# Scores of two heads issued together, a rounded forget bias, and fewer unread products in a softmax stage

## The reference

```python
# forgetting branch (per layer)
c = jnp.cumsum(log_f, axis=1).transpose(0, 2, 1)          # one row of 256 sums per head
z = jnp.einsum('bthd,bshd->bhts', q, k) * scale
z = z + cb[..., None] - c[:, :, None, :]                   # forget bias
p = jax.nn.softmax(jnp.where(causal, z, -jnp.inf), axis=-1)
...
# sparse branch (per layer)
z = jnp.einsum('btgrd,btkgd->btgrk', q, k_sel) * scale
p = jax.nn.softmax(jnp.where(valid, z, -jnp.inf), axis=-1)
...
# sliding-window attention (second block)
s = jnp.einsum('bnqkgd,bnskd->bnkgqs', q, kb) * (SWA_HEAD_DIM ** -0.5)
s = jnp.where(mask, s + bias, -jnp.inf)
p = jax.nn.softmax(jnp.concatenate([s, sink], -1), axis=-1)[..., :-1]
```

## Time and profile before

| | us |
|---|---|
| median of 3 runs | 2611.24 (2606.49 to 2626.17) |
| the profiled execution | 2605.32 |
| its span | 2603.5 |
| TensorE busy | 2487.0 (96%) |
| VectorE busy | 1755.4 (67%) |
| ScalarE busy | 1419.3 (55%) |
| mean granted TensorE clock | 0.977 |

### The profile page before, as it was taken

One profiled execution on the slowest core, in us unless ns is written; L12 is line 12 of the kernel. 1 busy time (PEld: TensorE's weight loads), 2 busy tenths in 40 slices (PEclk: granted clock), 3 DMA queues, 4 the chain that ended last, 5 costly groups with the idle time before them and its releaser, 6 DMA issues. The chain is left out here.

```text
span 2603.5 us, 34769 instructions
## 1 busy us (share of the span) xinstructions
PE 2487.0 (96%) x13881; PEld 2106.1 (81%) x13881; DVE 1755.4 (67%) x2013; ACT 1419.3 (55%) x1625; POOL 136.5 (5%) x176
## 2 busy tenths in 40 slices
PE   6999999999998999999999897999999999999996
PEld 6786789888866998878899786888888888888885
DVE  3345655544466555666544557898989898988987
ACT  3543544454345444523434445777777777777775
POOL 0101200001022000042000000000000000000000
PEclk9999999999999999899999997999999999999998
DMA  8232355532424455604555426999999999999996
GB/s 282 98 135 97 131 187 178 193 138 102 161 99 162 170 194 179 116 1 133 173 181 194 138 65 203 365 367 365 358 364 366 360 359 362 365 356 358 368 363 226
DMA packets 391569, 586.60 MB, mean 225 GB/s; under 512 B 21168, under 2 KB 284656, under 8 KB 391280
## 3 DMA queue, kind: packets, MB, share of 16 engines
q1 hardware_dynamic: 391408, 584.37, 66.3%
HBM read 580.13 MB, written 4.19 MB: 224 GB/s over the span
## 5 line engine op out<-in xcount | busy, mean ns | idle before, releaser
L3378 DVE TENSOR_TENSOR moe_low<-ring,moe_high 128x2048 fp32r<-128x2048 f32 x288 | 658.9, 2290 | 96.3 <-ACT moe_high L3339 92.4
L3339 ACT CAST moe_high<-ring 128x2048 fp32r<-128x2048 f32 x288 | 548.8, 1908 | 154.0 <-PE bank L3263 81.2
L3263 PE MATMUL bank<-moe_high,moe_xh 128*128 128x512 f32 x896 | 240.6, 390 | 7.9 <-PEq L3088 7.9
L3263 PE MATMUL bank<-moe_high,moe_xl 128*128 128x512 f32 x896 | 240.3, 390 | 0.0
L3263 PE MATMUL bank<-moe_low,moe_xh 128*128 128x512 f32 x896 | 240.1, 390 | 0.0
L3263 PEld LDWEIGHTS bank<-moe_high,moe_xh 128*128 128x128 f32 x896 | 168.4, 188 | 43.1 <-issue 8.1
L3263 PEld LDWEIGHTS bank<-moe_high,moe_xl 128*128 128x128 f32 x896 | 168.7, 188 | 35.2
L3263 PEld LDWEIGHTS bank<-moe_low,moe_xh 128*128 128x128 f32 x896 | 168.5, 188 | 35.1
L2048 DVE TENSOR_TENSOR chain_low<-ring,chain_high 128x2048 fp32r<-128x2048 f32 x48 | 110.0, 2292 | 127.3 <-ACT chain_high L2021 127.3
L2021 ACT CAST chain_high<-ring 128x2048 fp32r<-128x2048 f32 x44 | 83.8, 1904 | 151.9 <-PE bank L1992 116.9
L3269 PE MATMUL bank<-moe_high,moe_hh 128*128 128x512 f32 x448 | 128.4, 408 | 2.3 <-DVE moe_hl L3383 2.3
(11 more groups left out here) (513 smaller groups left out, 4993.6 us busy)
## 6 DMA issues: line engine op xcount, KB each, us to landing
ring<-in_moe_w_gate SPq DMA_DIRECT2D x199, 512.0 KB, 5.7
ring<-in_moe_w_up SPq DMA_DIRECT2D x199, 512.0 KB, 7.4
ring<-in_moe_w_down SPq DMA_DIRECT2D x95, 1024.0 KB, 7.9
ring<-in_w_in SPq DMA_DIRECT2D x22, 2048.0 KB, 8.0
ring<-in_w_down SPq DMA_DIRECT2D x14, 2048.0 KB, 7.9
ring<-in_w_up SPq DMA_DIRECT2D x10, 2048.0 KB, 8.1
xT<-in_moe_w_down SPq DMA_DIRECT2D x18, 1024.0 KB, 7.7
xT<-in_moe_w_gate SPq DMA_DIRECT2D x31, 512.0 KB, 5.7
```

The costliest lines, as they stand in the source:

```text
L3263: mm = pe.matmul(core.banks[i % 2][:], (xl if other_low else xh)[:, place(m), 4 * part + c, :], wt[:, c, :], start=(part == 0 and j == 0 a ...
L3339: act.copy(unit(high, u), ring.raw(u)).then_inc(s["weight_high"], 1)
L3378: dve.tensor_tensor(unit(low, u), ring.raw(u), unit(high, u), ALU.subtract)\
```

## The change

The scores of heads `i` and `i+1` are issued together on every even step: first both heads' products for the first 128 queries, then both for the second 128, so that neighbouring products use array rows 0 to 63 and 64 to 127 in turn. They wait until both banks are free. In the forget stage the two bias products of a half follow the two score products. A bias product is now of type fp32r with 72 array rows: the sums are held as three rounded parts (rows 0 to 7, 32 to 39, 64 to 71), and a matrix of zeros and ones, `thirds`, picks a head's three rows. VectorE makes those parts from 72 rows of sums, with four operations more at unit 21, two more at unit 17 and two more at unit 19. In the swa stage one unread product per step is left of four. `thirds` adds 8 columns to the constants, and `cum` has moved out of the arena.

The line numbers of the changed kernel are higher: L1180 are the scores, L1185 the bias products, L1079 the gate projection, L370 the unread products, L1200 the transposes, L1208 to L1210 the products with the values.

```diff
--- before.py
+++ after.py
@@ -44,7 +44,7 @@
 ARENA = 15232
-LOWER, UPPER, UPPER_BC = 7168, 6144, 5248
+LOWER, UPPER, UPPER_BC = 6976, 6144, 5248
 TRI = 3 * P
@@ -86,6 +86,7 @@
         "expert": np.tile(np.arange(E), (P, 1)),
+        "thirds": (p % 32 == np.arange(8)[None, :]) & (p < 72),
     }
@@ -1170,21 +1171,24 @@
         for i in range(heads + 3):
-            h = i
-            if h < heads:
-                if h >= 2:
-                    pe.wait_ge(s["masked"], h - 1)
-                bank = core.banks[h % 2]
+            if i < heads and i % 2 == 0:
+                both = (i, i + 1)
+                if i >= 2:
+                    pe.wait_ge(s["masked"], i)
                 for t, (a, b) in enumerate(edges):
-                    mm = pe.matmul(bank[:, a:b], q(h)[:, t * P:(t + 1) * P], k(h)[:, 0:b - a],
-                                   start=True, stop=(bias is None))
-                    if bias is not None:
-                        mm = pe.matmul(bank[:, a:b], bias_lhs(h), bias_rhs[:, 0:b - a], start=False, stop=True)
-                mm.then_inc(s["scores"], 1)
+                    for h in both:
+                        mm = pe.matmul(core.banks[h % 2][:, a:b], q(h)[:, t * P:(t + 1) * P], k(h)[:, 0:b - a],
+                                       start=True, stop=(bias is None))
+                        if bias is None and t == NT - 1:
+                            mm.then_inc(s["scores"], 1)
+                    for h in both if bias is not None else ():
+                        mm = pe.matmul(core.banks[h % 2][:, a:b], bias_lhs(h), bias_rhs[:, 0:b - a], start=False, stop=True)
+                        if t == NT - 1:
+                            mm.then_inc(s["scores"], 1)
             if logits is not None:
...
             if sink is not None:
-                idle_products(core, pe, core.banks[2 + i % 2][:, TRI:BANK], 4)
+                idle_products(core, pe, core.banks[2 + i % 2][:, TRI:BANK], 1)
             h = i - 2
@@ -1421,11 +1425,16 @@
     LOADS = 6
-
-    def __init__(self, core, rows, turned, fl, b, cum, tmp, logits):
-        self.core, self.rows, self.turned, self.fl, self.b, self.cum, self.logits = core, rows, turned, fl, b, cum, logits
+    ROWS = 72
+
+    def __init__(self, core, rows, turned, fl, b, cum, tmp, rest, logits):
+        self.core, self.rows, self.turned, self.fl, self.b, self.rest, self.logits = core, rows, turned, fl, b, rest, logits
         self.u, self.e = tmp[:, 8:24], tmp[:, 24:40]
-        self.u2 = self.u.rearrange("p (t h) -> p t h", t=NT)
+        self.u2, self.e2 = (a.rearrange("p (t h) -> p t h", t=NT) for a in (self.u, self.e))
+        self.flat = tmp[:, 40:40 + NT * self.ROWS]
+        self.spread = self.flat.rearrange("p (t h) -> p t h", t=NT)
+        self.bias = cum[0:self.ROWS, :]
+        self.pick = core.thirds[0:self.ROWS, :]
         self.s = {n: core.sem(f"first_{n}") for n in ("turned", "step", "log", "sums", "cum")}
@@ -1437,11 +1446,11 @@
         if u == 20:
-            pe.wait_ge(s["step"], 4)
-            bank = core.banks[6]
-            pe.matmul(bank[0:8, 0:P], self.u2[:, 0, :], core.const("le"), start=True, stop=True)
-            pe.matmul(bank[0:8, P:T], self.u2[:, 0, :], core.const("ones"), start=True, stop=False)
-            pe.matmul(bank[0:8, P:T], self.u2[:, 1, :], core.const("le"), start=False, stop=True).then_inc(s["sums"], 1)
+            pe.wait_ge(s["step"], 5 + 3)
+            bank = core.banks[6][0:self.ROWS]
+            pe.matmul(bank[:, 0:P], self.spread[:, 0, :], core.const("le"), start=True, stop=True)
+            pe.matmul(bank[:, P:T], self.spread[:, 0, :], core.const("ones"), start=True, stop=False)
+            pe.matmul(bank[:, P:T], self.spread[:, 1, :], core.const("le"), start=False, stop=True).then_inc(s["sums"], 1)
@@ -1475,13 +1484,25 @@
             dve.tensor_scalar(self.u, self.u, -1.0, 0.0, ALU.mult, ALU.max).then_inc(s["step"], 1)
+            dve.memset(self.flat, 0.0).then_inc(s["step"], 1)
+            dve.tensor_copy(self.pick, core.const("thirds")[0:self.ROWS, :]).then_inc(s["step"], 1)
         if u == 19:
-            dve.wait_ge(s["step"], 3)
+            dve.wait_ge(s["step"], 5)
             dve.wait_ge(s["log"], 2)
-            dve.tensor_tensor(self.u, self.u, e, ALU.add).then_inc(s["step"], 1)
+            for n in range(3):
+                dve.tensor_tensor(self.spread[:, :, 32 * n:32 * n + 8], self.u2, self.e2, ALU.add).then_inc(s["step"], 1)
         if u == 21:
+            sums = core.banks[6][0:self.ROWS, 0:T]
+            rest = self.rest[0:self.ROWS, :]
             dve.wait_ge(s["sums"], 1)
-            dve.tensor_copy(self.cum[0:8, :], core.banks[6][0:8, 0:T]).then_inc(s["cum"], 1)
+            dve.tensor_copy(self.bias, sums).then_inc(s["step"], 1)
+            dve.wait_ge(s["step"], 9)
+            dve.tensor_tensor(rest, sums, self.bias, ALU.subtract).then_inc(s["step"], 1)
+            dve.wait_ge(s["step"], 10)
+            dve.tensor_copy(self.bias[32:64, :], rest[32:64, :]).then_inc(s["step"], 1)
+            dve.tensor_copy(self.bias[64:72, :], rest[64:72, :]).then_inc(s["step"], 1)
+            dve.wait_ge(s["step"], 12)
+            dve.tensor_tensor(self.bias[64:72, :], rest[64:72, :], self.bias[64:72, :], ALU.subtract).then_inc(s["cum"], 1)
             self.logits.rest(dve, 0)
@@ -2106,7 +2127,7 @@
         lambda h, t: core.const("neg")[:, P * t:P + 2 * P * t], br,
-        bias=(lambda h: core.const("ident")[0:8, h:h + 1].broadcast_to([8, P]), cum[0:8, :]), logits=gates[0], rope=rope,
+        bias=(lambda h: side.pick[:, h:h + 1].broadcast_to([side.ROWS, P]), side.bias), logits=gates[0], rope=rope,
         behind=BehindProjections(of_projections, side, branches))
@@ -2133,25 +2154,27 @@
     br, at = core.part(at, NT, BW)
-    cum, at = core.part(at, T)
     tmp, at = core.part(at, 320)
+    rest, at = core.part(at, T)
     with core.scratch("upper_a", UPPER, LOWER):
...
-    with core.first_unit(f"attention{i}"), core.scratch("upper_bc", UPPER_BC, LOWER):
+    with core.first_unit(f"attention{i}"), core.scratch("upper_bc", UPPER_BC, LOWER), \
+            ExitStack() as memory:
+        cum = memory.enter_context(core.nc.sbuf_tensor(f"forget_sums{i}", [P, T], F32R))[:]
         parts = Parts(core)
...
         gates = [SplitLogits(core, "forget", w, base + 11, logits[1], 0, parts, 0, 0, led=True)]
-        side = FirstTurn(core, br, branches, core.cproj[:, :, 0:8], core.b_forget[:, i, :], cum, tmp, gates[0])
+        side = FirstTurn(core, br, branches, core.cproj[:, :, 0:8], core.b_forget[:, i, :], cum, tmp, rest, gates[0])
         projections, of_projections = split_projection_part(core, "bc_proj", w, [
...
             beside=lambda pool: clear(pool, sems), side=side)
-        later_branches(core, w, i, base, projections, of_projections, side, branches, br, qT, kT, v, cum, tmp, logits, gates,
+        later_branches(core, w, i, base, projections, of_projections, side, branches, br, qT, kT, v, tmp, logits, gates,
                        parts)
```

3 lines of the change are left out of this document (2 added, 1 removed).

## The result

| | before | after |
|---|---|---|
| median, us | 2609.35 (2606.49 to 2626.17, 4 runs) | 2524.86 (2522.13 to 2526.03, 4 runs) |
| the profiled execution, us | 2605.32 | 2525.50 |
| its span, us | 2603.5 | 2523.8 |
| TensorE busy, us | 2487.0 | 2405.0 |
| mean granted TensorE clock | 0.977 | 0.979 |

The ratio is 0.9664, with a 95% interval of 0.9628 to 0.9699: faster by 84.5 us. The terms are looked at first, then what lies outside them.

What follows compares the result with a forecast made beforehand. TensorE's list was taken to bound the forget, sparse and swa stages, and DMA the experts' part from about 1600 us. Savings of 21.1, 8.2 and 18.0 us sum to 47.3, giving 2564 us against the median 2611.2; range 2547 to 2590.

Steps and rivals of the forecast that it cites:

- The terms: Savings claimed per stage: forget stage 21.1 us in two layers, sparse stage 8.2 us in two layers, swa stage 18.0 us.
- the sum: Whole kernel: 21.1 + 8.2 + 18.0 = 47.3 us saved, giving 2564 us against the median 2611.2.
- The eight more columns of constants are nothing: Constants: the eight columns added were claimed to cost nothing.
- rival (2): Layer 0's forget stage: its 10.24 us half-clock stretch goes, 5.1 us, giving 2559 us; kept within the forecast, together 0.72.
- Two heads overlap: Score products, all five stages: the second head's scores cost only 0.01 to 0.02 us more.
- rival (3): Score pairs: the heads don't overlap in the new order, 15.4 us come back, 2579 us; chance 0.07.
- FirstTurn's chain is covered: Unit 21: four more VectorE operations, 2.0 us, hidden behind the last projection tile with 0.6 us to spare.
- Swa step 1.72 us, VectorE and TensorE tied: Swa stage: both engines' lists tied at 1.72 us a step, bounds 1.63 and 2.00; 18.0 us saved.
- Rival (1): Swa stage: clock falls to half with fewer unread products, stage 8 us longer than before, 2590 us; chance 0.12.
- Rival (4): Forget and sparse stages: another wait takes the place, half of their 29.3 us comes back, 2579 us; chance 0.07.
- Rival (5): All five changed stages: TensorE goes to 1.2 GHz, 2698 us, slower than before; chance 0.02.
- The rule on tiling modes: Forget pair: changing tiling mode drains the engine; four changes of 0.20 us within 1.92 us of scores and biases.

Runs made afterwards that it cites:

- the four layouts: Kernel before with only unused buffers added, giving the changed kernel's operand distance: 2581.0 to 2583.2 us at 120 us of half clock, against 2605.4.
- the window of 23.9 us above: Half-clock stretch in layer 1's forget stage, profiled run of the kernel before with activations' parts 64 bytes up; that kernel's median 2597.13 us, ratio 0.9928.

## Why the prediction was wrong

**The failed step is the sum, in what it left out.** "The eight more columns of constants are nothing" was a statement on time, and as such wrong: these 32 bytes and the 32 of `thirds` changed the distance between the operands of every rounded product of the activations' parts with the weights' parts. Some 4750 of these run outside the changed stages (1536 and 1056 at L2013, 1392 at L907, 768 at L917) and became faster by 5 or 6 ns each, 1032 of 512 columns by 3 ns: 27 to 32 us as an estimate from the paces, 23.0 by the four layouts, 22.7 by undoing it in the changed kernel at equal H. The last two are differences of measured times; why the paces give more is open. No row that I read had to do with it; the earlier trace rows show 0.12 us a product, and I took that as a constant of the operation.

**The second is a size: rival (2).** I counted 5.1 us for one stretch at half clock because one execution showed one of 10.24 us in a forget stage. The runs of before spend 130 us at half clock, those of after 106, and 24 x 0.431 = 10.3 us come from it. The execution that was profiled was a lucky one, at a clock of 0.977 against a usual 0.975. Half-clock stretches in the forget stages come and go between layouts and runs, as the earlier trace rows and the window of 23.9 us above show; the denser stage no longer has them.

**The terms held, each within about 3 us.** At H = 120, with the expectation by the prediction's terms beside it:

| step | measured | by the terms |
|---|---|---|
| placement | 23.0 | 0 |
| rounded bias, single heads (2582.4 to 2569.4) | 13.0 | 9.8 |
| two heads at once, all five stages (2569.4 to 2542.8) | 26.6 | 27.7 |
| three unread products a step fewer (2542.8 to 2530.0) | 12.8 | 9.8 |
| together | 75.4 | 47.3 |

With 10.3 us for the clock this is 85.7, measured 84.5. The 52.4 us of the change's own parts stand against 47.3 by the terms and 48.2 by the windows of the stages. The 4 us between the last two are in no window that changed, and four differences of means that are each good to about 2 us can't settle them.

**Point by point.** *Two heads overlap*: right, 0.85 us for eight records; rival (3) is out. *FirstTurn's chain is covered*: right, 1.96 us forecast as 2.0, with 0.84 us of VectorE idle behind it. *Swa step 1.72 us, VectorE and TensorE tied*: right, and the hundredth is luck, since the bounds were 1.63 and 2.00. *Rival (1)*: it did not happen. The reason I gave for that, that what remains is packed more densely, fits the one-unread-product kernel, where the clock falls without the pairs. The Trainium skill (TensorE: Matmul & The Clock Gate, Part 1) has the clock set by how busy TensorE has been recently. Read as the profile's busy share, the rule does not separate these runs: 0.50 over 71.7 us with 68.79 busy, and 1.00 in the changed kernel across waits of 1.18 and 1.19 us. *Rival (4)*: no other wait came. *Rival (5)*: out. *The rule on tiling modes* (the Trainium skill, TensorEngine Tiling (Array Packing), Key Properties): four drains a pair were counted, 0.20 us each. The trace agrees with a cost at each of the four, 0.21, 0.15, 0.20 and 0.10 us; scores and biases of a pair came out 0.16 us under the forecast.

## What to carry to other kernels

A change of a few bytes in an early buffer moves everything behind it, and can shift the pace of matmuls in stages that the edit never touches; after any edit that adds a buffer, compare the pace of an untouched group of products, and try the layout with one pad before crediting or blaming the edit. Correct each run for its time at half clock before reading small differences: here it explains nearly all of the scatter of one kernel (a standard deviation of 1.3 us left of 11.6). In this stage the filler products were needed with single heads of 64 rows and not with two heads together; so make the work dense first, then take the filler out, and look at the granted clock.

## What the runs showed of the hardware

- The pace of rounded products of 256 columns (128 x 128 weights) depends on where the two operands begin in SBUF relative to each other: 119 or 120 ns when they begin at the same place modulo 128 bytes, mostly 117 at 32 bytes on either side, 113 or 114 at 64, with single groups at up to 118. The MLP's products of 512 columns follow the distance modulo 256, from the weights to the activations: 227 ns at 0, 229 at 192, 232 at 128 and at 32, 234 at 224.
- Moving both operands together changes nothing: the experts' products with the activations, whose operands keep a distance of 0 modulo 256, go every 227 ns in every layout that was tried.
- An execution's time follows its time at half clock by 0.43 us for each us, over 62 runs. At half rate a stretch that TensorE bounds would give 0.5.
- TensorE can be busy for 68.79 of 71.70 us and stay at a granted clock of 0.50 all the while (single heads of 64 rows, one unread product).
- Why a forget stage with single heads and 8-row biases falls to half clock in one run and not in another was not found.
